# Norm gains moved to ScalarE, and level products summed by TensorE, in a hybrid decoder step

## What is computed

```
z   = rmsnorm(x, norm_mix) @ w_in                  # 3920 columns, split over two head groups
mla = latent attention, 8 heads, QK norm per head   # sample tokens: over a paged cache of 2048 past tokens
gla: b = cumsum(log_sigmoid(a) / 16); A[t,s] = sum_k q[t,k] k[s,k] exp(b[t,k] - b[s,k]), s <= t
     o = (q exp(b)) @ S0 + A @ v;   S = exp(b_last) S0 + (k exp(b_last - b)).T @ v      # 4 heads, 128 x 256
     y = rmsnorm(o, norm_gla_out) * silu(r)
h   = x + concat(rmsnorm(mla, norm_mla_out), y) @ w_out
h   = h + peer(rmsnorm(h, norm_ffn))                # 8 heads, top 16 of 16384 experts each
out = h + sigmoid(rmsnorm(h, norm_ple) @ w_ple_gate) * (p @ w_ple_proj)
```

## Time and profile before

| what | value |
|---|---|
| median of 3 runs | 4408.99 us (4402.73 to 4420.45) |
| profiled execution, its own time | 4402.15 us |
| span of its instructions | 4400.3 us |
| mean granted TensorE clock | 0.719 |
| busy: TensorE, VectorE, ScalarE, POOL | 2226.7, 3337.7, 490.1, 2235.1 us |
| moved by DMA | 1606.64 MB, mean 365 GB/s |

### The profile page before, as it was taken

How to read it: one execution, slowest core, us unless ns; L and a number is a source line. 1 busy time by engine, 2 the same in 40 slices (tenths; PEclk the granted TensorE clock), 3 DMA queues, 4 the chain that set the end, 5 groups by cost and what they waited for, 6 DMA issues and landing times.

```text
span 4400.3 us, 23443 instructions
## 1 busy us (share of the span) xinstructions
PE 2226.7 (51%) x8006; PEld 1309.9 (30%) x8006; DVE 3337.7 (76%) x3712; ACT 490.1 (11%) x917; POOL 2235.1 (51%) x1232
## 2 busy tenths in 40 slices
PE   8999715324898492789852438800000380000746
PEld 3456403213384131367641212800000130000312
DVE  0230699898568997968889865699999879987772
ACT  1220102221001001222112011000000100000000
POOL 0000365634232466567785742545768647877440
PEclk9999856557999796767765669955555695555877
DMA  8667889988998999889998999988899999999996
GB/s 309 235 228 283 332 345 357 362 330 323 420 419 342 412 423 384 349 328 367 395 392 326 363 389 421 401 347 328 369 414 389 400 422 422 422 404 422 421 396 213
DMA packets 262973, 1606.64 MB, mean 365 GB/s; under 512 B 28051, under 2 KB 50131, under 8 KB 92934
## 3 DMA queue, kind: packets, MB, share of 16 engines
q0 software_dynamic: 176448, 1268.30, 71.2%
q1 hardware_dynamic: 84518, 327.82, 19.7%
q10 hardware_dynamic: 1888, 9.03, 0.5%
HBM read 1561.93 MB, written 42.56 MB: 365 GB/s over the span
## 4 chain that ended last, share of the span: by engine, by line
PE 34%; DVE 30%; POOL 14%; DMA 12%; issue 7%; ACT 2%; another core or an unknown queue 0%; SPq 0%; DVEq 0%; ACTq 0%; POOLq 0%
PE bank L791 15%; POOL ring L2407 13%; DVE total L1890 10%; DVE ring L1865 10%; PE bank L1201 5%; DMA ring<-in_peer_u,idx_all 4%; PE bank L1164 4%; DMA ring<-in_peer_v,idx_all 4%; PE bank L845 1%; PE bank L765 1%; POOL front L2389 1%; PE bank L995 1%; PE bank L1035 1%; PE bank L1009 1%; PE bank L915 1%
## 5 line engine op out<-in xcount | busy, mean ns | idle before, releaser
L2407 POOL DMA_INDIRECT ring<-in_peer_v,idx_all x576 | 1086.7, 1887 | 747.5 <-DVE total L1890 346.3
L1865 DVE CUSTOM_DVE_ANT_0 ring<-ring,xrow 128x2048 f32<-128x2048 f32 x576 | 1298.5, 2286 | 205.8 <-DMA ring<-in_peer_u,idx_all 203.3
L1890 DVE SCALAR_TENSOR_TENSOR total<-ring,gate_all,total 128x2048 f32<-128x2048 f32 x571 | 1342.0, 2350 | 144.7 <-DMA ring<-in_peer_v,idx_all 119.5
L2407 POOL DMA_INDIRECT ring<-in_peer_u,idx_all x576 | 1050.7, 1824 | 756.0 <-DVE dots L1865 387.5
L791 PE MATMUL bank<-front 128*128 128x512 f32 (+3 forms) x2048 | 897.7, 596 | 76.4 <-ACT front L1996 71.8
L765 PE MATMUL bank<-ident,front 128*128 128x128 f32 (+1 forms) x320 | 61.8, 369 | 1375.5 <-DVE front L1290 1298.7
L791 PEld LDWEIGHTS bank<-front 128*128 128x128 f32 (+1 forms) x2048 | 357.2, 179 | 606.7 <-issue 602.1
L765 PEld LDWEIGHTS bank<-ident,front 128*128 128x128 f32 (+1 forms) x320 | 50.5, 201 | 1394.0 <-DVE front L1290 1295.2
L1164 PE MATMUL bank<-front 128*128 128x128 f32 (+2 forms) x1536 | 257.3, 330 | 11.1 <-DMA front<-in_peer_w_q 7.6
L1164 PEld LDWEIGHTS bank<-front 128*128 128x128 f32 x1536 | 241.0, 193 | 29.0 <-DMA front<-in_peer_w_q 11.4
L1201 PE MATMUL bank<-ring 128*128 128x490 f32 x384 | 165.6, 579 | 2.1 <-ACT front L1996 2.1
(11 more groups left out here) (305 smaller groups left out, 2806.8 us busy)
## 6 DMA issues: line engine op xcount, KB each, us to landing
front<-in_w_in SPq DMA_DIRECT2D x64, 980.0 KB
front<-in_w_out SPq DMA_DIRECT2D x48, 1024.0 KB
front<-in_peer_w_q SPq DMA_DIRECT2D x48, 1024.0 KB
front<-in_w_ple_gate SPq DMA_DIRECT2D x48, 1024.0 KB
ring<-in_w_in POOLq DMA_DIRECT2D x12, 1960.0 KB, 10.0
front<-in_w_uq SPq DMA_DIRECT2D x6, 1536.0 KB, 9.0
ring<-in_peer_u,idx_all POOLq DMA_INDIRECT x576
ring<-in_peer_v,idx_all POOLq DMA_INDIRECT x576
```

Source lines behind the costliest of these rows:

```text
L1865: e.tensor_tensor_reduce(out=ring[:, b, :], in0=ring[:, b, :], in1=xrow[:, t % 2, :], scale=1.0, scalar=0.0, op0=ALU.mult, op1=ALU.add, ac ...
L1890: e.scalar_tensor_tensor(out=total, in0=ring[:, b, :], scalar=c1, in1=total, op0=ALU.mult, op1=ALU.add).then_inc(s("summed"), 1)
L2407: e.indirect_dma_start(out=ring[:, k % RING, :], out_offset=None, in_=a[("peer_u", "peer_v")[side]][0], in_offset=bass.IndirectOffsetOnAxi ...
```

## The change

- **Norms other than ffn.** VectorE scales the identity by 1/rms into inv_diag (128x128) instead of the row. TensorE multiplies the raw row block by inv_diag where it transposed Y. ScalarE applies the gain, now one value for each partition from gains_t, in four 128-column activations instead of one copy of a bank. The broadcast loads of norm_mix, norm_mla_out, norm_ple and norm_gla_out go; one load of gains_t comes, ahead of the input rows on SyncE. The gain of the GLA output is part of the mix gains.
- **Level sums.** AT and its reduce go. TensorE multiplies each masked level by the values, 8 products into one accumulation for a prompt head, 4 for a sample head. am has two places. The order on TensorE becomes: products of heads 0 and 1, transposes of kd, then by head the products two heads on and the sums, and after all four the state updates. Banks move with it.
- **GLA output.** ScalarE squares the output in PSUM, and VectorE makes go in four 256-column operations from PSUM, with 1/rms and silu(r) in one.
- **Gains of keys.** The key's gain is folded into the query's once, at the start; L1382 and L1359 go.
- **Waits.** SyncE, ScalarE and POOL wait for nt_transposed in three places where they waited for normed; the output projection waits for gla_o_ready instead of gla_o_sb.
- **Lists.** All lists of the order are new. ROWS_BEFORE has 689 steps instead of 714, since the gone steps have no place in it.

```diff
@@ norm_transposes (TensorE)
-                            src = H[:R, sl, k * P:(k + 1) * P] if use == "mix" and k >= 8 else Y[:R, k * P:(k + 1) * P]
-                            mm = e.transpose(norm_bank(n, m)[:, j * P:j * P + R], src, ident[:R, :R])
+                            cols = slice(k * P, (k + 1) * P)
+                            row = Y[:R, cols] if use == "ffn" else in_rows(t)[:R, cols] if use == "x" else H[:R, sl, cols]
+                            out = norm_bank(n, m)[:, j * P:j * P + R]
+                            if use == "ffn" or use == "mix" and k >= KD // 2:
+                                mm = e.transpose(out, row, ident[:R, :R])
+                            else:
+                                mm = e.matmul(out, row, inv_diag[:R, :R], start=True, stop=True)
@@ norm_rows (VectorE)
+                    if use != "ffn":
+                        e.tensor_scalar(inv_diag[:R, :R], ident[:R, :R], inv, None, ALU.mult).then_inc(s("normed"), 1)
+                        yield
+                        continue
@@ norm_squares (ScalarE)
-                        e.copy(xt[:, 4 * q:4 * q + 4, sl * P:sl * P + R], four(norm_bank(n, m), R)).then_inc(s("nt_evacuated"), 1)
+                        if use == "ffn":
+                            ins = e.copy(xt[:, 4 * q:4 * q + 4, sl * P:sl * P + R], four(norm_bank(n, m), R))
+                        else:
+                            for j in range(4):
+                                k = 4 * q + j
+                                gain = gains_t[:, ("x", "mix", "ple").index(use), k:k + 1]
+                                ins = e.activation(xt[:, k, sl * P:sl * P + R], norm_bank(n, m)[:, j * P:j * P + R], ACT.Copy, scale=gain)
+                        ins.then_inc(s("nt_evacuated"), 1)
@@ linear_attention (TensorE)
+                    def intra(h, stop):
+                        u = t * H_GLA + h
+                        yield
+                        e.wait_ge(s("levels_masked"), u + 1)
+                        if t and h == 0:
+                            e.wait_ge(s("gla_o_ready"), t)
+                        ob = gla_out_at(t, h)[:R, (h % 2) * GV:(h % 2 + 1) * GV]
+                        am = masked_at(t, h)
+                        for n in range(NLEV - lv0):
+                            last = n == NLEV - lv0 - 1
+                            mm = e.matmul(ob, am[:R, n, 0:R], values(h), start=(n == 0), stop=(last and stop))
+                        mm.then_inc(s("levels_summed"), 1)
...
-                            e.matmul(ob, AT[:R, h, 0:R], vg, start=True, stop=(t == 0))
...
+                        for h in range(H_GLA):
+                            if h < 2:
+                                yield from products(h + 2)
+                            if h == 0:
+                                yield
+                                e.wait_ge(s("kdr_sb"), t + 1)
+                            yield from intra(h, t == 0)
+                            if t:
+                                ob = gla_out_at(t, h)[:R, (h % 2) * GV:(h % 2 + 1) * GV]
+                                e.matmul(ob, qe[:, h * P:h * P + R], S0[:, h, :], start=False, stop=True)
@@ gla (VectorE)
-                    link(e.tensor_reduce(AT[:R, h, 0:R], am[:R, 0:nl, 0:R].rearrange("p l n -> p n l"), AX, ALU.add))
...
-                e.tensor_copy(go[:R, 0:512], gla_out_at(t, 0)[:R, :])
-                e.tensor_copy(go[:R, 512:1024], gla_out_at(t, 2)[:R, :]).then_inc(s("gla_o_sb"), 1)
...
-                link(e.tensor_tensor(gv, gv, GIS[:R].unsqueeze(2).to_broadcast([R, H_GLA, GV]), ALU.mult))
-                link(e.tensor_tensor(gv, gv, g_go[:R, :].unsqueeze(1).to_broadcast([R, H_GLA, GV]), ALU.mult))
-                e.tensor_tensor(go[:R, :], go[:R, :], gsil[:R, :], ALU.mult).then_inc(s("gla_o_ready"), 1)
+                for h in range(H_GLA):
+                    cols = slice(h * GV, (h + 1) * GV)
+                    ins = e.scalar_tensor_tensor(out=go[:R, cols], in0=gla_out_at(t, h)[:R, (h % 2) * GV:(h % 2 + 1) * GV],
+                                                 scalar=GIS[:R, h:h + 1], in1=gsil[:R, cols], op0=ALU.mult, op1=ALU.mult)
+                ins.then_inc(s("gla_o_ready"), 1)
@@ mixer (VectorE)
-                    link(e.tensor_tensor(krow[:, :, :], krow[:, :, :], g_k[:, 0:NOPE].unsqueeze(1).to_broadcast([P, HH, NOPE]), ALU.mult))
```

More of the change, by code:

```diff
@@ L462, in gla_out_at, with gla_update_at @@
         def gla_out_at(t, h):
[L463 removed]
+            return bank[(4 if t in GROUPS[0] else 6) + h // 2]
+        def gla_update_at(t, h):
+            return bank[(h % 2) * (2 if t in GROUPS[0] else 4)][:, 0:GV]
         def first_slot(u, side):
@@ L673, in residual_rows @@
                         e.dma_start(H[:ROWS[t], slot(t), :], x_rows(t)).then_inc(s("rows_loaded"), 16)
-                    e.wait_ge(s("normed"), NORMS["mix", tiles[-1]] + 1)
                     e.dma_start(G, down(a["norm_ffn"][0])).then_inc(s("gain_loaded"), 16)
@@ L1099, in linear_attention, with products @@
                     e.wait_ge(s("level_done"), level_count(t, NLEV - 2) + 1)
-                    for h in range(H_GLA):
+                    def products(h):
                         u = t * H_GLA + h
@@ L1112, in linear_attention, with values @@
                         mm.then_inc(s("level_products"), 1)
+                    def values(h):
+                        return gz[:R, 2 * H_GLA * GK + h * GV:2 * H_GLA * GK + (h + 1) * GV]
+                    def intra(h, stop):
[10 more added lines that the diff above has]
+                        mm.then_inc(s("levels_summed"), 1)
+                    yield from products(0)
+                    yield from products(1)
                     yield
@@ new lines, in linear_attention @@
+                        for b in range(DEC_B):
+                            mm = e.matmul(ob, qz[:, b, :], Ss[h % 2][:, b, :], start=False, stop=(b == DEC_B - 1))
+                        mm.then_inc(s("gla_out_psum"), 1)
+                        for b in range(DEC_B):
+                            mm = e.matmul(bank[b // 2][:, (b % 2) * GV:(b % 2 + 1) * GV], kz[:R, b, :], values(h),
+                                          start=True, stop=True)
+                        mm.then_inc(s("sample_state_psum"), 1)
@@ L1991, in z_rows @@
                 else:
-                    e.wait_ge(s("normed"), NORMS["x", tiles[-1]] + 1)
+                    e.wait_ge(s("nt_transposed"), 4 * (NORMS["x", tiles[-1]] + 1))
                 for sl, t in enumerate(tiles):
@@ L2426, in _ @@
                 if n == AHEAD_BUFS - 1:
-                    e.wait_ge(s("normed"), NORMS["x", GROUPS[AHEAD][-1]] + 1)
+                    e.wait_ge(s("nt_transposed"), 4 * (NORMS["x", GROUPS[AHEAD][-1]] + 1))
                 if n >= AHEAD_BUFS:
```

120 lines of the change are left out of this document (59 added, 61 removed), and 69 rows, old and new, of tables (CHAIN_BEFORE_PIECE, ROWS_BEFORE).

## The result

The change takes 4442.71 us (median of 5 runs, 4439.07 to 4447.71) where the kernel before takes 4408.99 (its median too is of 5 runs, not of 3). The ratio is 1.007, with a 95% interval of 1.0054 to 1.0086: slower by 0.7%, some 31 us by the ratio and 34 by the medians. The forecast was 4385 us, in a range of 4350 to 4425. It was wrong in sign and outside its range.

The account below looks back on a forecast made before the run. TensorE was taken to bound the time before the first gather, then VectorE in three stages and DMA in the others. Terms +12 - 2 - 26 - 7 - 1 = -24 us gave 4385 us against the median, range 4350 to 4425.

Parts of the forecast that it names:

- Before the first gather: Up to POOL's first row gather: TensorE's additions less the moved pieces' credit, gather at 488, +12 us.
- The sum up to the 96th piece: TensorE's full stretch up to the 96th ahead piece: level sums +12.0, turns +4.4, first norm -0.4, total +16 us.
- turns and first norm: On the way to the 96th ahead piece: 40 transposes become products, +4.4 us; the first norm's scaling changes, -0.4 us.
- Stage 1: Gated attention tiles 1 and 2: VectorE's saved 27.6 us go into rows taken earlier as the chain lengthens, -2 us.
- The sample attention: Sample attention steps, code unchanged by the change: the prediction has no term for them.
- Stage 2 without the sample attention: Tiles 3 and 4: VectorE's savings of 26.5 us count where it bounds the stage, -26 us; bounds 0 to -26.5.
- DMA: Broadcast gain loads that go: two PLE ones -5, the last group's input one -2; -7 us, between 0 and -10.
- The end: Closing chain: scaling -2.1, first bank's evacuation in four pieces +0.5, products at the low clock +0.4; -1 us.
- The exposed level sums: Rival: in tiles 1 and 2 the sums' 47.7 us all stand on the chain at row 239; 4433 us, chance 0.10.
- the lists only shift work: Rival: the hand-written order misses the new durations, so VectorE gains nothing, -2 and -26 go; 4413 us, chance 0.03.
- the rule weighed in the prediction: Fp32 transposes four times faster than products: 40 turns cost 13 us, not 4.4, gather at 497; 4394 us, chance 0.02.

Follow-up runs that it names:

- e1: The whole computation of the change under the five order lists of the kernel before: 4435.97 us, ratio 1.0063.
- e3: The kernel before with the level sums on TensorE alone, under its own order lists: 4425.76 us, ratio 1.0042.
- e8: The kernel before's order with the norm weights on ScalarE alone, level sums on VectorE and the longer output kept: 4414.68 us, ratio 1.0026.
- e12: The change in its own order, but with the old rows and old page list in the sample attention's steps: 4428.90 us, ratio 1.0036, on another chip.
- e4: The computation of the kernel before, unchanged, under the five order lists of the change: 4484.31 us, ratio 1.0177.
- e11: The change in its own order with the next tile's columns loaded ahead of the stores: 4433.86 us, ratio 1.0061.
- e2: The change without its level sums (VectorE adds the levels), under the order lists of the kernel before: 4426.39 us, ratio 1.0046.
- e6: The change under the order lists of the kernel before, with the next tile's columns loaded ahead of the stores: 4406.29 us, ratio 0.9992.
- e7: The kernel before with only the earlier load of the next tile's columns, no new TensorE wait: 4404.89 us, ratio 0.9998.

## Why the prediction was wrong, step by step

**Before the first gather: +12 forecast, +24.7 measured.** The sum up to the 96th piece was right: +16 forecast, +16.1 at e1's gather, under the old order (level sums 12.0 forecast and 11.9 in e3; turns and first norm +4.4 - 0.4 forecast and 3.0 in e8, so a microsecond of the agreement is luck. The -0.4 is mis-added: its own terms, -2.35 + 0.27 + 0.43 + 1.5, give -0.15). The rest, 8.6 us, is the first step that failed: "The lists now put some ten ahead pieces behind the head's last scores instead of before them", with a credit of up to 4 us ("its exponentials no longer stand on ScalarE ahead of the copies", and the wait for the route gone). Moving them left TensorE 7.40 us idle ahead of tile 0's mix norm. The route did come earlier than under the old order (483.3, e1 490.3), and waited for the pieces. e1, with the old list, has the gather at 492.2.

**Stage 1: -2 forecast, 0 measured** (24.7 at the gather, 24.6 at tile 2's top-k). Right, and the reason given (the time goes into rows taken earlier) fits. Where no rows were moved the savings bought nothing either: in e1 they met 15.4 us of waits for the products.

**The sample attention: put at nothing, +23 measured.** The largest step that failed is a missing term. The prediction read the lists at the gated attention and the norms, and priced nothing for the steps between, whose code is unchanged. Rows and pages move against these steps. Putting both back took 14 us of the 23 away (e12); the new order on the old computation added 20 (e4). Both figures are from single profiles; against the middle of the old order's runs the new order costs 11 to 14. The rest has no cause shown: the stage moved by up to 10 us in runs that changed nothing in it.

**Stage 2 without the sample attention: -26 forecast, -11 measured.** Tiles 3 and 4 gave some 20 us by the output of tile 4. Then 9 us were lost up to the mix norm. There VectorE waited for a row gather 9.5 us in one piece (14.4 us in all), beside the output projection's weights and the mix rows; that these delayed it is only argued, as no run took them away. "Bounds: 0 if the gathers can't come faster, -26.5 if they can" left out the third case that decided the old order's runs: VectorE reaches a step that hangs on a trip through memory. In e1 it had won 8 us by tile 3's output and paid 16 at tile 4's gate. "A microsecond off VectorE counts in three of the stages" was read from a mean over the stage, which hides such a step. The new order fills that gap with 14 rows instead of 8, which is why the change itself does not show the wait and e11 gains 1.5 us at that gate.

**DMA: -7 forecast, about -4 measured.** The 7 MB did go. Between tile 4's last route and the last PLE norm the delay falls from 40.0 to 36.4 (with 21 rows fewer taken at the first, so the 40.0 hangs on the rate). Under the old order, where no rows need counting, it falls from tile 2's PLE norm to tile 4's by 5.3 us in e8 (14.4 to 9.1) and by 6.3 in e2, and not at all in e3, which moves the bytes of before (22.4 and 22.4). So the term had the right sign and size, though e8 and e2 also take 2 us off VectorE at each of these norms, and nothing parts the two.

**The end: -1 forecast, +4 measured.** The step is "the products at the low clock +0.4". The last norm's 16 turns, before and after (32 instructions after, as each product is two):

```profile
4326.98 2.26 PE L765 MATMUL bank<-ident,front 64*128 64x64 f32 x16 [99.41 <-DVE front L1290]
```

```profile
4361.31 7.09 PE L782 MATMUL bank<-inv_diag,front 64*128 64x64 f32 x32 [93.14 <-DVE inv_diag L1333]
```

At the granted clock of 0.50 they take 7.09 us for 2.26: +4.8, or 0.30 a turn. The prediction's +0.4 is what four turns add at the full clock (0.11 each).

**The rivals.** The exposed level sums were the slow case, with 48 us in tiles 1 and 2. It did not happen so: VectorE waited there 1.0 us for the products in the change and 15.4 in e1, and the delay at tile 2's first top-k was that of the first gather in both. The case "the lists only shift work" had 0.03; it is the nearest, but it was priced as a gain missed (4413) and not as a loss. The prediction treated the new order as a thing that can only fail to help.

**Turns.** Eight turns by a plain product took 1.95 us in e8 at the high clock, 0.244 each, against 0.11 for a transpose: a factor of two. By the rule weighed in the prediction (the Trainium skill, TensorE: Matmul & The Clock Gate, Terms) it would be four, and by the prediction's estimate from that factor the first gather of e8 would come some 13 us late; it is 3.0. The trace disagrees there. At the end of the kernel, with 64 columns at the low clock, the factor is 3.1.

## What to carry to other kernels

In this program, whose engines run written orders, time saved on the busiest engine was lost at the next step that hangs on a trip through memory and other engines. List such trips with the time from store to load before crediting a saving, and move the load ahead of the store (e6: 30 us where the engine came early; e7: nothing where it did not). Taking the trip away made the change level, not faster: 81 us less work on VectorE was worth no more than that. And when order lists change with the computation, price each stretch that they reorder, code unchanged or not, and measure computation and order apart: here +30 us for the one, 3 to 7 for the other on top of it, and +78 for the new order on the old computation. A stage compared between two single profiles wants a third: this one moved by 10 us without a change in it.

## What the runs showed of the hardware

Issues by size and us to landing, in the kernel before (2390 to 2402 us), then in e1 (2390 to 2430 us):

```profile
front<-z_dram SPq DMA_DIRECT2D x1, 772.0 KB, 6.2
mix_dram<-front SPq DMA_DIRECT2D x1, 512.0 KB, 2.7
out_gla_p<-front SPq DMA_DIRECT2D x1, 512.0 KB, 3.8
```

```profile
front<-z_dram SPq DMA_DIRECT2D x1, 772.0 KB, 10.9
mix_dram<-front SPq DMA_DIRECT2D x1, 512.0 KB, 9.3
out_gla_p<-front SPq DMA_DIRECT2D x1, 512.0 KB, 17.4
```

At the same step, a 512 KB store landed in 2.7 us in the kernel before, at a DMA share of 0.57, and in 9.3 in e1, at 1.00; the next one took 3.8 and 17.4, the 772 KB load behind them 6.2 and 10.9. (In e6, where the load goes first, it took 9.7 and the stores 7.6 and 17.7.) The wait for these stores was thus 4 us in the one and 18 in the other; the row gathers beside them are the difference that the rows show. ScalarE's scaled copy of a 128x128 bank piece took 0.378 us on average where a plain copy took 0.280. And turning a transpose into a product was dearest where TensorE had idled before: 16 turns of 64 columns took 4.8 us more at 1.2 GHz (0.30 each), where 128 columns in a full stretch took 0.11 more each.
